# Two matrix products in seven blocks, and triangular inverses that move between array halves, in a two-block f32 network

## The chip, the cores and the metric

The program runs on one core of one Trainium2 chip, all in f32. The metric is the device time of one execution in microseconds (us). The kernel before took 2334.2, 2336.51 and 2338.58 us in three runs, median 2336.51. Engines are named as in the profile: PE is TensorE (PEld its weight loads), DVE is VectorE, ACT is ScalarE, POOL is GpSimd, SP is the engine that issues most transfers.

## The reference, cut to what matters

The network has two blocks, each of two layers, on 256 tokens of width 1024. The first block's layer is a feed-forward, a hybrid mixer and another feed-forward; the change touches the mixer:

```python
def rg_lru(u, w_a, b_a, w_x, b_x, lam):       # u: 256 x 1280, ten heads of 128
    r = sigmoid(u @ w_a per head + b_a); i = sigmoid(u @ w_x per head + b_x)
    log_a = -8.0 * r * softplus(-lam)
    a = exp(log_a)
    mult = sqrt(-expm1(2.0 * log_a))
    # h_t = a_t h_{t-1} + mult_t * (i_t u_t)
    ...
def hybrid_mixer(h, ...):
    ...
    y_pool = pool_mixer(u_pool, ...) @ w_pool_up                       # 512 -> 1024
    y_lru = (rg_lru(v, ...) * gelu(u_gelu)) @ w_lru_up                 # 1280 -> 1024
    return (g_pool * y_pool + g_lru * y_lru) @ w_out                   # 1024 -> 1024
```

The second block's first layer is a delta-rule recurrence with 16 heads of 64, run forwards and backwards over 256 context and 256 latent tokens:

```python
    def step(S, inp):                         # S: 64 x 64 for each head
        r_t, w_t, k_t, v_t, kk_t, a_t = inp
        sa = einsum("bhvk,bhk->bhv", S, kk_t)
        S = S * w_t - outer(sa, kk_t * a_t) + outer(v_t, k_t)
        return S, einsum("bhvk,bhk->bhv", S, r_t)
```

Its second layer is differential attention, which the change doesn't touch.

## The kernel before, in words

**First block.** Weights lie in one tensor in the order of use and come as slots of 16 tiles of 128 x 128 (1 MB, issued by SP) into a ring of 5. TensorE goes through them in that order and writes to 8 PSUM banks, which a list (`Order`, here `FIRST`) deals out by the place in the program; each entry names the engine that empties it. Three kinds of product stand there: plain ones (`st.product`, L704: one weight tile against 256 tokens), and in the feed-forwards products of 2 x 2 blocks of weight tiles in seven multiplications instead of eight, each with 128 tokens (L1080 the first matrix, L1141 the second). For these VectorE adds up four sums of weight tiles per slot (`sum_slot`, S1 to S4, L2373 to L2376) and three combinations of the data; `add_down` (L2532 to L2542) puts the seven results together and adds them into x. In the mixer all is plain: the order is the w_in columns, the gates' products by head (`gate_a`, `gate_x`), then `pool_up` (8 outputs of 4 products), `lru_up` (8 of 10), `w_out` (8 of 8). VectorE runs the recurrence head by head (`recurrence(h)`, L2594 to L2605) with the decay worked out from a tanh of ScalarE by a reciprocal, then adds up y.

**The scan of the second block.** 32 turns (`TURNS`): 8 pairs of heads, 4 groups each (`GROUPS`). A turn q takes for both directions two chunks of 64 tokens: four units u of (chunk, direction), for two heads h. Head h = 0 lives on partitions 0 to 63, h = 1 on 64 to 127 (`halves`), and all its products of 64 x 64 run in the quadrant of the array with these rows and these columns. In each turn a unit needs the inverse of a triangular 64 x 64 matrix. It starts from the Gram products (`first_gram`), which VectorE copies under a mask over ones laid by ScalarE (`begin_inverse` after `lay_ones`), and doubles in levels 1 to 5: `lower_product` (L1343, 8 products), VectorE's mask (`mask_lower`, L2814), `next_inverse` (L1354 and L1356, 16 products, 8 in level 5), ScalarE's copy back (`take_inverse`, L1992). Levels 1 and 2 of turn q+1 are done within turn q, beside the levels 3 to 5 of turn q. The chain of the state goes between them: for each of the two chunks k of the turn before `state_product` (L1421, L1433), VectorE's `take_z`, `solve`, ScalarE's `take_u`, `out_and_state` (L1447 to L1456), `update_state` and `take_o`. Also `stacked_gram` (L1330, L1331), once a turn, and three side tiles for the pair ahead or behind ("middle": in q = 0 mod 4 the `spread` of kk_norm, L1364; "kv": L1391; "end": `low_rank` L1377 or `by_head` L1371).

The order on each engine is written out by hand in one loop over q per engine; a wait holds up all that stands behind it there. Once a pair VectorE makes the decay sums of the next pair (`sum_decays`, L2726, behind `mask_lower(q, 5)`), and each turn it transposes the v squares (`turn_squares`, L2800 and L2805), which SP then writes to memory and reads back turned for the `kv` products of the next turn (its wait is on `v_landed`, L1387).

## Time and profile before

| | |
|---|---|
| runs | 2334.2, 2336.51, 2338.58 us |
| profiled execution | 2333.88 us, span 2331.8 us |
| PE busy | 2298.4 us, 99% |
| DVE busy | 1541.3 us, 66% |
| ACT busy | 547.4 us, 23% |
| the chain that ended last | PE 92%, DVE 3%, ACT 3%, DMA 1% |
| of that, lines of PE | L704 28%, L1080 21%, L1141 12%, L1354 3%, L1343 2%, L1356 2% |

The span is the time between the first and the last recorded instruction; the execution's own time is 2.1 us longer. An f32 matmul leaves two records. Matmuls overlap in the pipeline, so the mean duration of one says little, and the pace is read from starts. In the view of time a row is a run of like instructions: start, the time that they took together, their line and shape (rows*columns of the array, then the written tile), and in brackets the idle time before with what ended it.

### The profile page before, as it was taken

To read this page: it belongs to the slowest core of one execution; us is meant where nothing else is said; L and a number is where in the kernel's file an instruction comes from. 1 tells how busy PE (TensorE), PEld (TensorE's weight loads), DVE (VectorE), ACT (ScalarE), POOL (GpSimd) and SP (SyncE) were. 2 spreads that over 40 slices of the span, in tenths; PEclk is the share of its full clock that TensorE was granted. 3 is DMA by queue.
4 is the path that set the end of the run, shared out by engine and by line. 5 is a ranking of instruction groups with operands and counts; after the bars stand their busy time and mean duration, and the time that the engine had idled before them with its cause. 6 is when DMAs were issued, how large, how long until landed. Compare 5 with 4: busy or idle time off the path is not lost.

```text
span 2331.8 us, 55763 instructions
## 1 busy us (share of the span) xinstructions
PE 2298.4 (99%) x24340; PEld 2011.3 (86%) x24340; DVE 1541.3 (66%) x3133; ACT 547.4 (23%) x1280; POOL 413.9 (18%) x483
## 2 busy tenths in 40 slices
PE   8999999999999999999999999999999999999999
PEld 8999888899999998888999988668888889456558
DVE  7886775388768866671897887446666666147552
ACT  2101030111011000301110201225555554032341
POOL 1111000011111200000123440025445451100000
PEclk9999999999999999999999999999999999999999
DMA  7555454445545554544555421113333334212212
GB/s 284 195 181 192 171 197 145 163 166 195 200 170 192 182 199 145 217 151 158 184 194 181 145 91 73 37 27 62 61 59 59 60 61 100 98 56 89 73 37 73
DMA packets 169458, 310.29 MB, mean 133 GB/s; under 512 B 108992, under 2 KB 134768, under 8 KB 135296
## 3 DMA queue, kind: packets, MB, share of 16 engines
q1 hardware_dynamic: 165024, 278.02, 36.4%
q0 software_dynamic: 4192, 28.72, 3.4%
q8 instruction: 192, 3.15, 0.6%
q14 instruction: 50, 0.41, 0.1%
HBM read 293.06 MB, written 13.63 MB: 132 GB/s over the span
## 4 chain that ended last, share of the span: by engine, by line
PE 92%; DVE 3%; ACT 3%; DMA 1%; issue 1%; SPq 1%; POOL 0%; DVEq 0%; ACTq 0%; POOLq 0%
PE psum L704 28%; PE psum L1080 21%; PE psum L1141 12%; PE psum L1249 6%; PE psum L722 6%; PE psum L1354 3%; PE psum L1343 2%; PE psum L1356 2%; PE psum L1451 1%; PE psum L1051 1%; PE psum L1447 1%; PE psum L1377 1%; DVE arena L2814 1%; PE psum L1612 1%; PE psum L1654 1%
## 5 line engine op out<-in xcount | busy, mean ns | idle before, releaser
L704 PE MATMUL psum<-arena,ring 128*128 128x256 f32 (+1 forms) x2864 | 674.7, 395 | 8.3 <-ACT arena L1758 8.0
L704 PEld LDWEIGHTS psum<-arena,ring 128*128 128x128 f32 x2864 | 541.4, 190 | 129.5 <-issue 56.4
L1080 PE MATMUL psum<-arena 128*128 128x128 f32 x2560 | 325.0, 275 | 0.0
L1080 PEld LDWEIGHTS psum<-arena 128*128 128x128 f32 x2560 | 305.1, 192 | 0.0
L1080 PE MATMUL psum<-arena,ring 128*128 128x128 f32 x1920 | 253.6, 275 | 0.0
L1080 PEld LDWEIGHTS psum<-arena,ring 128*128 128x128 f32 x1920 | 233.9, 192 | 0.2
L2373 DVE TENSOR_TENSOR arena<-ring 128x1024 f32<-128x1024 f32 x136 | 171.0, 1258 | 38.7 <-PE psum L1141 34.8
L1141 PE MATMUL psum<-arena 128*128 128x128 f32 x1408 | 184.6, 275 | 0.0
L1141 PEld LDWEIGHTS psum<-arena 128*128 128x128 f32 x1408 | 170.7, 192 | 0.0
L1354 PE MATMUL psum<-arena 64*64 64x64 f32 x2560 | 162.1, 222 | 7.2 <-DVE arena L2814 5.3
L2395 DVE SCALAR_TENSOR_TENSOR arena<-arena 128x256 f32<-128x256 f32 x336 | 164.0, 529 | 5.1
L1354 PEld LDWEIGHTS psum<-arena 64*64 64x64 f32 x2560 | 142.7, 133 | 27.8 <-DVE arena L2814 17.9
L1141 PE MATMUL psum<-arena,ring 128*128 128x128 f32 x1056 | 146.0, 275 | 0.0
L722 PE MATMUL psum<-arena,ring 128*128 128x512 f32 (+1 forms) x336 | 137.9, 555 | 0.0
L1356 PE MATMUL psum<-arena 64*64 64x64 f32 x2048 | 134.8, 218 | 0.0
L1141 PEld LDWEIGHTS psum<-arena,ring 128*128 128x128 f32 x1056 | 131.4, 192 | 0.1
L2814 DVE TENSOR_TENSOR arena<-psum,arena 128x256 f32<-128x256 f32 x160 | 67.8, 424 | 88.4 <-PE psum L1343 83.9
L1783 ACT ACTIVATE arena<-arena 128x256 f32<-128x256 f32 x88 | 36.7, 417 | 370.3 <-DVE arena L2511 343.6
L1356 PEld LDWEIGHTS psum<-arena 64*64 64x64 f32 x2048 | 122.1, 135 | 0.0
L1992 ACT ACTIVATE arena<-psum 128x512 f32<-128x512 f32 x128 | 76.3, 597 | 150.6 <-PE psum L1356 149.9
L722 PEld LDWEIGHTS psum<-arena,ring 128*128 128x128 f32 x336 | 61.3, 189 | 53.6 <-issue 50.1
L1343 PE MATMUL psum<-arena 64*64 64x64 f32 x2560 | 104.8, 220 | 1.0 <-ACT arena L1992 0.9
(338 smaller groups left out, 3372.7 us busy)
## 6 DMA issues: line engine op xcount, KB each, us to landing
ring<-in_weights SPq DMA_DIRECT2D x238, 1024.0 KB, 4.8
arena<-in_ada POOLq DMA_DIRECT2D x24, 1024.0 KB, 5.2
squares<-arena SPq DMA_DIRECT2D x128, 96.0 KB, 2.1
arena<-squares SPq DMA_DIRECT2D x128, 64.0 KB, 2.8
arena<-squares SPq DMA_DIRECT2D x128, 32.0 KB, 2.3
arena<-in_const POOLq DMA_DIRECT2D x1, 1312.0 KB, 6.7
arena<-in_x SPq DMA_DIRECT2D x1, 1024.0 KB, 4.8
ring<-in_weights SPq DMA_DIRECT2D x2, 512.0 KB, 6.6
```

The source lines that it names most:

```text
L704: mm = self.nc.tensor.matmul(out, self.ring[:, slot % RING, i * P:(i + 1) * P], rhs, start=(kc == 0), stop=(kc == len(moving) - 1))
L722: mm = self.nc.tensor.matmul(out, self.ring[:, slot % RING, i * P:(i + 1) * P], rhs, start=start, stop=stop)
L1080: mm = nc.tensor.matmul(bank[:, n * P:(n + 1) * P], left[:, kind, pair, :], right[:, pair, :], start=(n == 0 and pair == 0), stop=(n == la ...
L1141: mm = nc.tensor.matmul(out_[name][:, n * P:(n + 1) * P], left[:, kind, place, :], right[:, pair, :], start=(n == 0 and pair == 0), stop=( ...
L1249: mm = nc.tensor.matmul(out_[:, n * T:(n + 1) * T], left[:, kind, pair, :], right[:, pair, :], start=(n == 0 and pair == 0), stop=(closes ...
L1343: mm = mm_(ps_t[b][halves[h], u, :], lt_all[halves[h], b, u, :], xy[halves[h], b, 0, u, :], start=True, stop=True)
L1354: mm = mm_(ps_xy[b][halves[h], 1, u, :], t_, y_, start=True, stop=True)
L1356: mm = mm_(ps_xy[b][halves[h], 0, u, :], y_, t_, start=True, stop=True)
L1992: ins = nc.scalar.activation(xy[:, b, :, :, :], ps_xy[b], ACT.Copy)
L2373: link(tt(sum_[:, S1:S3 + 1, :], w[:, W22:W11 + 1, :], w[:, W21:W21 + 1, :].to_broadcast([P, 2, QUADS * P]), ALU.add))
L2395: ins = stt(sum_, ada_[:, b, kc, :], weight, sum_, ALU.mult, ALU.add)
L2814: tt(t_low[:, b, :, :], ps_t[b], mask(f"below{level}"), ALU.mult).then_inc(s.t_masked[b], 1)
```

## The change

**The mixer's `lru_up` and `w_out`** are computed in seven multiplications for eight, as the feed-forwards' second matrices: 20 quadruples of weight tiles (2 x 2 tiles) for `lru_up`, 16 for `w_out`, four quadruples to a slot. VectorE makes nine more slot sums per layer (`sum_mixer_weights`), three combinations of hs, and per unit of two outputs those of y; the seven results of a unit of `lru_up` are put together in a new function `lru_up(unit)`, one of them copied by ScalarE first, those of `w_out` by `add_down`. The padding tiles of the mixer's weights stand ahead of `lru_up` and no longer behind `w_out`. ScalarE computes the decay a itself (an Exp for each head, ahead of the tanh), and `recurrence` is without its reciprocal and two TENSOR_SCALARs.

**The scan.** For odd q the inverses move: the result of a level is written to the other half's partitions (`half_of`), so its products have rows of one half and columns of the other, where those of even turns stay in their own. `first_gram` writes level 1 so; `begin_inverse` of an odd turn therefore copies the lower matrix twice, once to each half (two more copies of 64 x 256), and ScalarE's second laying of ones is twice as wide for it. A new `next_inverses` issues level 4 of turn q and level 1 of q+1 in alternation, and so level 5 and level 2. The order of the turn is new on TensorE, VectorE and ScalarE.

```diff
+    def half_of(q, level, h):
+        return h if q % 2 == 0 else (h + level) % 2
...
                 for u in range(4):
                     for h in range(2):
-                        mm = mm_(ps_t[b][halves[h], u, :], lt_all[halves[h], b, u, :], xy[halves[h], b, 0, u, :],
-                                 start=True, stop=True)
+                        at = halves[half_of(q, level, h)]
+                        mm = mm_(ps_t[b][at, u, :], lt_held[held][at, u, :], xy[at, b, 0, u, :], start=True, stop=True)
...
+            def inverse_product(q, level, i, u, h):
+                b, at, to = q % 2, halves[half_of(q, level, h)], halves[half_of(q, level + 1, h)]
+                y_, t_ = xy[at, b, 1, u, :], t_low[at, b, u, :]
+                left, right = (t_, y_) if i else (y_, t_)
+                return mm_(ps_xy[b][to, i, u, :], left, right, start=True, stop=True)
...
+            def next_inverses(q, level, level_ahead):
+                pe.wait_ge(s.t_masked[q % 2], level_count(q, level))
+                pe.wait_ge(s.t_masked[(q + 1) % 2], level_count(q + 1, level_ahead))
                 for u in range(4):
...
+                    for i in (1, 0):
+                        for h in range(2):
+                            if i or level < LEVELS - 1:
+                                mm = inverse_product(q, level, i, u, h)
+                        for h in range(2):
+                            mm_ahead = inverse_product(q + 1, level_ahead, i, u, h)
...
                     first_gram(q + 1)
+                lower_product(q, 3)
                 if k >= 0:
                     state_product(k)
-                lower_product(q, 3)
                 stacked_gram(q)
+                next_inverse(q, 3, range(0, 2))
                 if k >= 0:
                     solve(k)
-                next_inverse(q, 3)
+                next_inverse(q, 3, range(2, 4))
+                if ahead:
+                    lower_product(q + 1, 1)
                 if k >= 0:
                     out_and_state(k)
+                lower_product(q, 4)
                 side(q, "middle")
-                lower_product(q, 4)
                 if ahead:
-                    lower_product(q + 1, 1)
-                next_inverse(q, 4)
+                    next_inverses(q, 4, 1)
...
                 if k >= 0:
                     state_product(k + 1)
+                side(q, "kv")
+                lower_product(q, 5)
                 if ahead:
-                    next_inverse(q + 1, 1)
-                lower_product(q, 5)
+                    lower_product(q + 1, 2)
                 if k >= 0:
                     solve(k + 1)
-                side(q, "kv")
+                side(q, "end")
                 if ahead:
-                    lower_product(q + 1, 2)
-                next_inverse(q, 5)
+                    next_inverses(q, 5, 2)
...
                 if k >= 0:
                     out_and_state(k + 1)
-                side(q, "end")
-                if ahead:
-                    next_inverse(q + 1, 2)
...
+                if b:
+                    for h in range(2):
+                        nc.vector.copy_predicated(lt_held[2][halves[h], :, :], mask_bits("earlier")[halves[h], :, :],
+                                                  ps_first[b][halves[1 - h], 1, :, :])
...
-                    link(ts(scr[:, 0, :], t, 1.0, None, ALU.add))
-                    link(nc.vector.reciprocal(scr[:, 1, :], scr[:, 0, :]))
-                    ts(scr[:, 2, :], scr[:, 1, :], 2.0, -1.0, ALU.mult, ALU.add)
...
+                for i, units in enumerate(LRU_PLAN + OUT_PLAN):
+                    if i + SUM_BUFFERS - 1 < MIXER_SUMS:
+                        sum_mixer_weights(i + SUM_BUFFERS - 1)
+                    for unit, pairs in units:
+                        if i < len(LRU_PLAN):
+                            if pairs[-1][1] == LRU_PAIRS - 1:
+                                lru_up(unit)
+                        elif pairs[-1][1] == OUT_PAIRS - 1:
+                            add_down(unit, s.x_mixed, "w_out")
```

TensorE in a turn with q = 0 mod 4, from the last products of level 3 on. Before, L1354 and L1356 are the two products of `next_inverse`, L1447, L1451 and L1456 `out_and_state`, L1364 the side tile in the middle, L1343 `lower_product`:

```order
L1356 MATMUL psum<-arena 64x64
L1447 MATMUL psum<-ring,arena 64x64 x4
L1451 MATMUL psum<-arena 64x64 x4
L1456 MATMUL psum<-arena 64x64 x4
L1364 MATMUL psum<-arena 64x128 x8
L1343 MATMUL psum<-arena 64x64 x16
L1354 MATMUL psum<-arena 64x64
L1356 MATMUL psum<-arena 64x64
```

In the new kernel L1420 is `inverse_product`, L1412 `lower_product`, L1523 `solve`, L1537, L1541 and L1546 `out_and_state`, L1454 the side tile, L1511 `state_product`, L1481 the `kv` tile:

```order
L1420 MATMUL psum<-arena 64x64 x8
L1412 MATMUL psum<-arena 64x64 x8
L1537 MATMUL psum<-ring,arena 64x64 x4
L1541 MATMUL psum<-arena 64x64 x4
L1546 MATMUL psum<-arena 64x64 x4
L1412 MATMUL psum<-arena 64x64 x8
L1454 MATMUL psum<-arena 64x128 x8
L1420 MATMUL psum<-arena 64x64 x32
L1511 MATMUL psum<-arena,ring 64x64 x4
L1481 MATMUL psum<-arena 64x64 x8
L1412 MATMUL psum<-arena 64x64 x16
```

`lower_product(q+1, 1)` now stands ahead of `out_and_state`, and where two groups of 16 inverse products stood apart there is one of 32.

VectorE at the beginning of an odd turn's inverse, before: L2832 is `take_z`, L2814 the mask of level 3, L2786 and L2787 the copies under a mask of `begin_inverse`, L2822 the masks of the stacked Gram products, L2847 and L2860 `update_state`:

```order
L2832 TENSOR_TENSOR arena<-psum,arena 128x128
L2814 TENSOR_TENSOR arena<-psum,arena 128x256
L2786 COPY_PREDICATED arena<-arena,psum 128x512
L2787 COPY_PREDICATED arena<-arena,psum 128x256
L2822 TENSOR_TENSOR arena<-psum,arena 128x4x128 x2
L2814 TENSOR_TENSOR arena<-psum,arena 128x256
L2847 SCALAR_TENSOR_TENSOR arena<-psum,arena 128x64 x2
L2860 TENSOR_SCALAR arena<-arena 128x64 x2
```

And in the new kernel, where L2995 is `take_z`, L2977 the mask, L2944, L2948 and L2950 `begin_inverse`, L2985 the stacked masks:

```order
L2977 TENSOR_TENSOR arena<-psum,arena 128x256
L2995 TENSOR_TENSOR arena<-psum,arena 128x128
L2944 COPY_PREDICATED arena<-arena,psum 128x512
L2948 COPY_PREDICATED arena<-arena,psum 64x256 x2
L2950 COPY_PREDICATED arena<-arena,psum 128x256
L2977 TENSOR_TENSOR arena<-psum,arena 128x256
L2985 TENSOR_TENSOR arena<-psum,arena 128x4x128 x2
L2977 TENSOR_TENSOR arena<-psum,arena 128x256
L3010 SCALAR_TENSOR_TENSOR arena<-psum,arena 128x64 x2
L3023 TENSOR_SCALAR arena<-arena 128x64 x2
```

The two half copies are new (L2948), `take_z` comes behind the mask of level 3, and the mask of level 1 for the turn ahead comes right behind `begin_inverse`, ahead of the stacked masks.

## Rows read from the trace of the kernel before

**Rows 1.** The page: busy time by engine, and the granted clock in 40 slices.

```profile
PE 2298.4 (99%) x24340; PEld 2011.3 (86%) x24340; DVE 1541.3 (66%) x3133; ACT 547.4 (23%) x1280; POOL 413.9 (18%) x483
PEclk9999999999999999999999999999999999999999
```

**Rows 2.** The chain of waits in order of time: start, length, what ran.

```profile
318.33 138.75 PE psum L704 x640
...
466.18 125.06 PE psum L1080 x1120
```

**Rows 3.** View of time, PE, the scan: stacked Gram products that open a turn.

```profile
1661.37 0.32 PE L1331 MATMUL psum<-ring 64*64 64x128 f32 x1
...
1664.47 0.45 PE L1447 MATMUL psum<-ring,arena 64*64 64x64 f32 x8 [0.96 <-ACT arena L2005]
...
1676.17 0.32 PE L1331 MATMUL psum<-ring 64*64 64x128 f32 x1
...
1689.70 0.32 PE L1331 MATMUL psum<-ring 64*64 64x128 f32 x1
...
1717.47 0.32 PE L1331 MATMUL psum<-ring 64*64 64x128 f32 x1
```

**Rows 4.** View of time, DVE, feed-forward: a slot sum, and the end of `add_down`.

```profile
469.73 1.22 DVE L2373 TENSOR_TENSOR arena<-ring 128x1024 f32<-128x1024 f32 x1
470.98 0.69 DVE L2375 TENSOR_TENSOR arena<-arena,ring 128x512 f32<-128x512 f32 x1
...
663.71 0.42 DVE L2540 TENSOR_TENSOR arena<-arena,psum 128x256 f32<-128x256 f32 x1 [1.78 <-PE psum L1141]
...
664.37 0.41 DVE L2542 TENSOR_TENSOR arena<-arena,psum 128x256 f32<-128x256 f32 x1
```

**Rows 5.** View of time, ACT and DVE, the recurrence.

```profile
317.76 4.22 ACT L1822 ACTIVATE arena<-arena 128x256 f32<-128x256 f32 x10
...
329.74 1.75 DVE L2597 RECIPROCAL arena<-arena 128x256 f32<-128x256 f32 x1
```

**Rows 6.** View of time, PE: the tile kk_norm, and one level of an inverse.

```profile
1665.36 1.05 PE L1364 MATMUL psum<-arena 128*64 128x128 f32 x16
...
1682.44 0.34 PE L1354 MATMUL psum<-arena 64*64 64x64 f32 x4
...
1683.42 0.57 PE L1343 MATMUL psum<-arena 64*64 64x64 f32 x13
```

**Rows 7.** View of time, PE: stacked Gram products on all four quadrants.

```profile
1676.34 0.28 PE L1330 MATMUL psum<-ring 64*64 64x64 f32 x4
...
1676.55 0.27 PE L1331 MATMUL psum<-ring 64*64 64x128 f32 x1
```

**Rows 8.** View of time, ACT: what stands around the laying of ones.

```profile
1660.71 1.28 ACT L1934 ACT_TABLE_LOAD   x1
...
1663.17 0.63 ACT L1949 ACTIVATE arena<-arena 128x512 f32<-128x512 f32 x1
1663.68 0.41 ACT L1951 ACTIVATE arena<-arena 128x256 f32<-128x256 f32 x1
```

**Rows 9.** View of time, DVE: decay sums, transposes, `begin_inverse`.

```profile
1670.82 2.33 DVE L2726 TENSOR_TENSOR_SCAN arena<-arena 128x512 f32<-128x512 f32 x2
...
1673.38 0.44 DVE L2800 STREAM_TRANSPOSE arena<-ring 128x256 f32<-128x256 f32 x1
...
1677.51 0.75 DVE L2786 COPY_PREDICATED arena<-arena,psum 128x512 f32<-128x512 int32 x1 [0.55 <-ACT arena L1951]
1678.14 0.44 DVE L2787 COPY_PREDICATED arena<-arena,psum 128x256 f32<-128x256 int32 x1
```

**Rows 10.** View of time, PE and DVE: `kv` products, and the last transpose before them.

```profile
1627.91 0.47 PE L1391 MATMUL psum<-arena 64*64 64x64 f32 x9 [0.57 <-DMA arena<-squares]
...
1674.26 0.27 DVE L2805 STREAM_TRANSPOSE arena<-arena 128x128 f32<-128x128 f32 x1
...
1683.95 0.27 PE L1391 MATMUL psum<-arena 64*64 64x64 f32 x1
```

More of the change, by code:

```diff
@@ L195, with quad_plan @@
 assert DOWN_UNITS * DOWN_PAIRS % QUADS == 0
-def down_plan():
+def quad_plan(slots, pairs_of_unit):
     plan = []
-    for i in range(DOWN_SLOTS):
+    for i in range(slots):
         units = {}
         for place in range(QUADS):
-            unit, pair = divmod(i * QUADS + place, DOWN_PAIRS)
+            unit, pair = divmod(i * QUADS + place, pairs_of_unit)
             units.setdefault(unit, []).append((place, pair))
@@ L352, in first_order @@
                 o.add((lay, "pool_mix", m), "dve")
-        for name in ("pool_up", "lru_up", "w_out"):
-            for m in range(DC):
-                o.add((lay, name, m), "dve")
+        for m in range(DC):
+            o.add((lay, "pool_up", m), "dve")
+        for name in ("lru_up", "w_out"):
+            for unit in range(MIXER_UNITS):
+                o.add((lay, name, unit, "first"), "dve")
+                o.add((lay, name, unit, "second"), "dve")
         feed_forward(lay, "ffn2", 2 * lay + 1)
@@ L770, in build @@
     half_b = keep.take(4 * DC)
+    log_a = keep.take(LAYERS * LH)
     s_state = keep.take(2, HEAD)
@@ L1829, in _ @@
                     nc.scalar.activation(gl[:, m, :], gl[:, m, :], ACT.Sigmoid).then_inc(s.g_done, 1)
+                for unit in range(MIXER_UNITS):
+                    name = lay, "lru_up", unit, "first"
+                    act.wait_ge(s.bank_full, FIRST.full(name))
+                    if unit >= 2:
+                        act.wait_ge(s.lru_p1_added, lay * MIXER_UNITS + unit - 1)
+                    nc.scalar.activation(u_pad[:, unit % 2, PAD:PAD + P], psum[:, FIRST.bank(name), 0:P],
+                                         ACT.Copy).then_inc(s.lru_p1_copied, 1)
                 feed_forward("ffn2", 2)
@@ L2236, in _ @@
                 if lay == last:
-                    pool.wait_ge(s.dve_taken, FIRST.taken((last, "w_out", DC - 1)))
+                    pool.wait_ge(s.dve_taken, FIRST.taken((last, "w_out", MIXER_UNITS - 1, "second")))
                     pool.dma_start(xx[:, :, 0:T], ctx_in).then_inc(s.context_loaded, 16)
@@ new lines, in _ @@
+                forms_of([[hs_of[:, :, k, half, :] for half in range(2)] for k in range(2)],
+                         [hs_forms[:, i] for i in range(3)]).then_inc(s.hs_forms_ready, 1)
+                sum_mixer_weights(0)
+                for m in range(DC):
+                    pool_up(m)
+                    if m == DC // 2 - 1:
+                        sum_mixer_weights(1)
+                for i, units in enumerate(LRU_PLAN + OUT_PLAN):
+                    if i + SUM_BUFFERS - 1 < MIXER_SUMS:
+                        sum_mixer_weights(i + SUM_BUFFERS - 1)
+                    for unit, pairs in units:
+                        if i < len(LRU_PLAN):
[3 more added lines that the diff above has]
+                            add_down(unit, s.x_mixed, "w_out")
@@ L3035 @@
         part.extend(tiles(a["w_pool_up"][l]))
-        part.extend(tiles(a["w_lru_up"][l]))
-        part.extend(tiles(a["w_out"][l]))
         part.append(np.zeros((MIXER_PAD, P, P), np.float32))
+        part.extend(quadruples(tiles(a["w_lru_up"][l])))
+        part.extend(quadruples(tiles(a["w_out"][l])))
         feed_forward("ffn2")
```

198 lines of the change are left out of this document (148 added, 50 removed).

## The prediction, made before the changed kernel ran

> **What bounds the kernel now.** I read the page first. TensorE is busy for 99% of the span at the full granted clock, VectorE for 66%, ScalarE for 23% [rows 1]. So an edit pays only if it shortens TensorE's stream or a wait of it. Next I read the chain of waits in order of time, which tells two kinds of place apart. In the first block (to about 1310 us) it is TensorE alone in long unbroken pieces: 640 records in 138.75 us, 1120 in 125.06 [rows 2]. There the length is a count times a pace. An f32 product leaves two records, so a product with 256 moving columns costs 2 x 138.75/640 = 0.434 us, one with 128 columns 2 x 125.06/1120 = 0.2233 us. In the scan over 32 turns (1554 to 1990 us) the view of time shows short pieces and many hand-overs. Four turns last 56.10 us there: stacked Gram products begin at 1661.37, 1676.17, 1689.70 and, two turns on, 1717.47 [rows 3], so the turns take 14.80, 13.53 and twice 13.9 us. Real waits of TensorE there are few (0.96 us at 1664.47 is among the longest), but each level of an inverse is product, mask on VectorE, product, copy on ScalarE, so the other engines' order decides as soon as TensorE gets shorter.
>
> **The mixers' last products.** Per layer 80 + 64 = 144 products of 256 columns go, 144 x 0.4336 = 62.4 us. In come 36 quadruples x 7 = 252 products of 128 columns, 252 x 0.2233 = 56.3 us. Two layers: -12.2 us, all of it on the chain.
>
> What has to hide beside it, per layer: VectorE gets nine slot sums (1.25 from the start of the first addition to that of the second, then 0.73 twice: 2.7 us each), four units of adding and forming at about 4.4 us (14 links of 0.2 to 0.46 us, from the same operations at 128 and 256 columns), and four additions into x at 3.0 us [rows 4]. A slot of 28 products lasts 28 x 0.2233 = 6.25 us, and a sum with four fifths of a unit is 6.2 us. That is full, but the first sums are made during pool_up, some 9 us ahead, and by my count the lead only falls to 6. The tightest place is the change from lru_up to w_out: unit 3's forms are ready about 4.0 us after the last lru_up product, and the 21 products put ahead of the ones that need them last 4.7 us. I take 0; at worst 1 us a layer. Into the next feed-forward the chain is that of ffn2 into the second layer's ffn1, where x is ready 1.1 us after the products [rows 4] and the row of the chain shows no wait of weight. Slots are used every 6.25 us where it was 16 x 0.4336 = 6.94, as in the feed-forwards, where the same ring keeps up.
>
> The recurrence loses a reciprocal of 1.75 us [rows 5] and two short operations per head. ScalarE gets ten exponentials ahead of the tanh (4.2 us, like its ten Tanh [rows 5]), so the first root is 4.2 us later, 6.8 with two more table loads of 1.28 [rows 8]. TensorE runs eight banks ahead there, about 18 us, so both cost 0.
>
> **The scan: what leaves TensorE.** A turn has 16 products in each of the inverses' levels 1 to 4, 8 in level 5. On two quadrants 32 records take 0.98 us (1682.44 to 1683.42), 29 to 30 ns each [rows 6], so 58 ns per quadrant. Now level 4 of turn q runs with level 1 of q+1, and level 5 with level 2, on four quadrants. If the quadrants don't hinder each other, two of 0.93 us become one, and 0.47 + 0.93 becomes 0.93: -1.40 us a turn. No row shows four equal streams. The nearest is the stacked Gram: 11 records begin between 1676.33 and 1676.55 on all four quadrants, 20 ns each [rows 7]. At 20 ns the 64 records take 1.28 us. Bounds for the first merged group: 0.93 (free) and 1.87 us (no concurrency). I take 1.05, between free and the Gram's pace.
>
> **The scan: what comes late in its place.** I laid one turn out, with T the last record of the merged products that end the turn before. Hand-overs, as I read them off the starts of such pairs: 0.26 us from a last start to VectorE or ScalarE, 0.05 back. I go through a turn with q = 0 mod 4, like the one at 1661. ScalarE copies both inverses and the output and is free at T+1.4. Then come the gates of the pair ahead (table load and two, 2.45 us up to 1663.17) and the ones (0.52 + 0.41) [rows 8]; for an odd turn ahead the second lay is twice as wide, so it ends at T+5.0. VectorE then begins the odd inverse: 0.64 + 0.43 as before [rows 9], and two half-array copies, not shown before, between 0.1 and 0.44 each; I take 0.33, by the 128x256 one. That is done at T+6.8. The product that waits for it, lower_product(q+1, 1), stands now ahead of out_and_state(k), where TensorE arrives at T+4.7; before it stood one group (1.0 us) and a tile later. So here 2.1 us are waited, and behind it queue out_and_state (0.89 from 1664.47 to 1665.36 [rows 3, 6], and 0.15 for the switch of tile shape), lower_product(q, 4) 0.48, the tile kk_norm 1.1 [rows 6], and the merged products end at T+10.9. From there: state 0.24, kv, ScalarE's copy 0.26 + 0.60 + 0.05, two lower products 0.97, solve 0.24, the end tile 1.2, merged 0.95: 4.3 us. Total 15.2 against 14.80. The same count gives 13.5 against 13.9 for q = 2 mod 4 (exponentials of 1.3 us before the ones, no middle tile; wait for the stacked masks and the level-4 mask) and 13.5 against 13.9 for q = 3 (square root with its load ahead of the begin).
>
> For q = 1 mod 4 the inverses alone would allow 12.6. But in the turn before, the two decay scans (2.33 us) now stand behind the mask of level 2, and the transposes (1.15 us) behind them [rows 9]: squares_turned comes at T+1.7, where it now comes 0.1 us before the turn's start. The v squares go out to memory and back. In one turn TensorE waited 0.57 us for them (1627.91); in another they were there at most 9.4 us after the last transpose (1674.53 to 1683.95, no wait) [rows 10]. I take 8.7, a little under that, so T+10.4; TensorE would be at kv at T+8.8. It waits 1.6 us, of which 0.3 was stall anyway: 13.9 against 13.53.
>
> Four turns: 15.2 + 13.9 + 13.5 + 13.5 + 4 x 0.12 for the merged pace = 56.6 against 56.1; seven such groups +3.5, and the last pair, whose side tiles are missing, -2. The scan stays where it is, +1.5 us. Bounds: if v lands in time and the quadrants are free, 7 x -2.2 and -2, about -17; if neither, see the rivals.
>
> **Sum.** The profiled execution took 2333.88 us, its span 2331.8 and 2.1 around it. 2333.9 - 12.2 + 1.5 = 2323.2. It lay 2.6 us under the median of the three runs (2336.51, from 2334.2 to 2338.58), so the median should come to about 2325.
>
> A rule of the Trainium skill speaks against the merging. The page TensorE: Matmul & The Clock Gate, section "Wait — 56ns, not 53.3ns?", says "Start-to-start never drops below ≈25 ns however small N is". By it 64 merged records take 1.6 us and 48 take 1.2, so the scan would end 25 us later than in my sum and the kernel near 2350. The trace doesn't bear it out for f32 on quadrants (20 ns each over 11 records), but it has no such stretch longer than a microsecond.
>
> **Rivals.**
> - The scan gains too (0.20): v lands before kv, and the masks' chain is shorter than I count. For it: several of my waits overlap. Against: VectorE and ScalarE must do more in odd turns. 12 to 17 us less: 2308 to 2315.
> - Four quadrants don't run together (0.13), so that the change doesn't do what it says: TensorE issues at its present 29 ns. Then the pairs cost 1.87 and 1.40 us again, 1.3 us a turn more than in my sum, 31 turns: +40; part of it hides the waits I count, so 2345 to 2362, slower than before. It decides from about 23 ns per record: +0.42 + 0.17 us a turn is 18 us, which eats the mixers' gain. For it: no row shows the pace; against: the Gram rows.
> - The odd turn's begin costs more (0.13): ScalarE's queue ahead of the ones or the half copies are longer, by 0.3 to 0.6 us a turn: +9 to +19, so 2334 to 2344, about no change.
> - The mixers' gain is eaten by VectorE (0.06), which falls behind by 1 us a slot: 9 sums x 2 layers, 2330 to 2341.
>
> **Chances.** My forecast has 0.48, from 2318 to 2331. 0.2% is 4.7 us, about what a measurement can tell from no change. Faster by more (under 2331.8): the forecast, the first rival and a little of the last, 0.70. Within: most of the last two, 0.15. Slower: 0.15. The range is 2308 to 2340.
>
> **What would show it.** Right: pieces of 224 ns products, 56 us, where 62 us stood in both mixers, VectorE's sums well ahead; merged groups of 64 records in 1.0 to 1.1 us; a wait before lower_product(q+1, 1) in even turns of 0.4 to 2 us; kv waiting for a DMA in turns 1 mod 4; four turns in 56 to 57 us. Wrong: merged groups of 1.3 us or more, kv never waiting, four turns under 54 or over 58, or a wait between lru_up and w_out.

## The result: slower by 0.3%, and the profile after

The changed kernel takes 2343.0 us in the median (20 runs, 2336.57 to 2348.87), the kernel before 2334.19 (20 runs, 2331.39 to 2338.58): 1.0034 of the time before, 95% interval 1.0025 to 1.0042. Forecast were 2325 us and a range of 2308 to 2340. Its runs also lie farther apart, 12 us from the lowest to the highest for 7.

The first block gained what was forecast, all but half a microsecond. In the chain of waits of the changed kernel `quad_products` (L1214) stands in one piece in each layer, as long as worked out (56.3):

```profile
390.18 56.28 PE psum L1214 x504
...
1037.44 56.28 PE psum L1214 x504
```

The scan's first stacked Gram products begin at 1542.24 us for 1553.96 before, 11.7 us earlier. The scan lost it, and more: its 31 turns from there to the last stacked Gram take 445.6 us for 426.0. The page's busy row shows it from TensorE's side, with 97% of the span for 99% [rows 1]:

```profile
PE 2267.8 (97%) x24772; PEld 1989.1 (85%) x24772; DVE 1594.7 (68%) x3288; ACT 557.1 (24%) x1310; POOL 416.5 (18%) x483
```

The same four turns as in [rows 3], by the view of time of TensorE (L1398 is now `stacked_gram`): 57.45 us for 56.10.

```profile
1654.41 0.32 PE L1398 MATMUL psum<-ring 64*64 64x128 f32 x1
...
1669.93 0.32 PE L1398 MATMUL psum<-ring 64*64 64x128 f32 x1
...
1684.95 0.32 PE L1398 MATMUL psum<-ring 64*64 64x128 f32 x1
...
1711.86 0.32 PE L1398 MATMUL psum<-ring 64*64 64x128 f32 x1
```

What ends TensorE's waits, from the view of waits for TensorE alone over the scan (total, times, longest). Before:

```profile
PE psum L1447 <- ACT arena L2005: 6.0, 11, 1.0
PE psum L1354 <- DVE arena L2814: 4.7, 8, 1.3
PE psum L1391 <- DMA arena<-squares: 1.2, 2, 0.6
PE psum L1343 <- ACT arena L1992: 0.5, 1, 0.5
```

And after:

```profile
PE psum L1412 <- DVE arena L2950: 23.2, 18, 2.6
PE psum L1481 <- DMA arena<-squares: 17.8, 9, 3.1
PE psum L1420 <- DVE arena L2977: 8.4, 15, 1.0
PE psum L1397 <- issue: 2.5, 1, 2.5
```

12.4 us of waits have become 53 (with three small rows not shown). Two make it up: `lower_product(q+1, 1)` (L1412) waits for the last copy of `begin_inverse` (L2950), and the `kv` products (L1481) for the v squares. Turn 8 and turn 9 show both, and the merged group between them, in TensorE's view of time:

```profile
1659.15 0.68 PE L1412 MATMUL psum<-arena 64*64 64x64 f32 x16 [2.60 <-DVE arena L2950]
...
1662.25 1.16 PE L1420 MATMUL psum<-arena 64*64 64x64 f32 x64
1663.23 0.22 PE L1511 MATMUL psum<-arena,ring 64*64 64x64 f32 x2
...
1675.78 0.45 PE L1511 MATMUL psum<-arena,ring 64*64 64x64 f32 x8
1679.15 0.62 PE L1481 MATMUL psum<-arena 64*64 64x64 f32 x14 [2.92 <-DMA arena<-squares]
```

The merged group works: 64 records begin from 1662.25 on and the next product at 1663.23, 15 ns a record for the 29 of [rows 6]. The median over the scan is 0.94 us from first to last start. How the two waits arise stands on VectorE, whose rows answer to [rows 9] and [rows 10]:

```profile
1657.01 0.72 DVE L2944 COPY_PREDICATED arena<-arena,psum 128x512 f32<-128x512 int32 x1 [1.82 <-ACT arena L2055]
1657.75 0.89 DVE L2948 COPY_PREDICATED arena<-arena,psum 64x256 f32<-64x256 int32 x2
1658.65 0.44 DVE L2950 COPY_PREDICATED arena<-arena,psum 128x256 f32<-128x256 int32 x1
...
1665.65 2.33 DVE L2882 TENSOR_TENSOR_SCAN arena<-arena 128x512 f32<-128x512 f32 x2
...
1668.76 0.27 DVE L2968 STREAM_TRANSPOSE arena<-arena 128x128 f32<-128x128 f32 x1
```

VectorE stands idle for 1.82 us until ScalarE has laid the ones (L2055), and only then makes four copies; a half copy takes as long as one over all partitions (0.45 us). The transposes stand behind the decay sums and end at 1669.03. Then SP's queue sends the squares out and, 4.7 us later, fetches them:

```profile
1669.12 1.79 SPq L1052 DMA_DIRECT2D squares<-arena  x4
1673.79 6.36 SPq L1062 DMA_DIRECT2D arena<-squares  x8
```

The `kv` products wait for the first four of the eight fetches. These are back 10.0 us after the transposes, at 1679.0.

A third loss I had not thought of: the granted clock. The kernel before has it at 1.00 all through the scan. In the changed kernel it is at half in 8 of 31 turns (the profile's clock times the length of each turn gives 34.5 us at 1.2 GHz), each time behind one of these waits or the stall of L1397. Turn 20, one with a wait of 2.4 us that begins at 1830, by windows (PEclk is the third column from the end):

```profile
1831.00:1834.50 3.50, 2.11 (x36) 1.99 (x38) 2.25 (x6) 0.01 (x1) 0.00 (x0) 0.61 0.23 34
1834.50:1836.00 1.50, 1.50 (x28) 1.26 (x24) 0.68 (x2) 0.97 (x2) 0.00 (x0) 0.50 0.53 83
1836.00:1838.00 2.00, 2.00 (x22) 1.67 (x24) 0.81 (x3) 0.35 (x1) 0.00 (x0) 0.50 0.39 61
```

This turn takes 18.1 us, where turns 12 and 24 with much the same wait (2.6 us) and a full clock take 15.4. The Trainium skill (TensorE: Matmul & The Clock Gate, section "HAM oscillation — how this bites in real kernels") tells of a clock that falls to half when TensorE runs idle for want of data and costs time beyond the wait; this trace agrees, with idle pieces of 1.8 to 3.1 us ahead of such stretches, though not behind every one: of the scan's 12 idle pieces of 1.8 us or more, 8 are followed by half clock and 4 are not (turns 8, 9, 12 and 24).

The single runs point the same way. Of the changed kernel's 20 runs the five with a mean granted clock of 0.993 or more took 2336.6 to 2340.2 us, the ten with 0.991 or less 2341.1 to 2348.9. That alone doesn't show which is the cause, since a longer wait lengthens a run and lowers its clock.

### The profile page after: what moved, and what is told of

It is laid out like the page before. It is cut to its first block, busy times and chain, and to the rows that moved or that the text cites. A ratio compares the mean times of both kernels' runs of the same rounds, so it can differ in the third digit from the quotient of the medians.

```text
span 2340.9 us, 56946 instructions
## 1 busy us (share of the span) xinstructions
PE 2267.8 (97%) x24772; PEld 1989.1 (85%) x24772; DVE 1594.7 (68%) x3288; ACT 557.1 (24%) x1310; POOL 416.5 (18%) x483
## 4 chain that ended last, share of the span: by engine, by line
PE 87%; DVE 6%; DMA 3%; ACT 2%; SPq 2%; issue 1%; POOL 0%; DVEq 0%; POOLq 0%
PE psum L718 22%; PE psum L1115 21%; PE psum L1176 12%; PE psum L1315 6%; PE psum L736 6%; PE psum L1214 5%; PE psum L1412 3%; PE psum L1420 2%; DMA squares<-arena 1%; DMA arena<-squares 1%; SPq L1062 1%; PE psum L1086 1%; PE psum L1481 1%; DVE arena L2500 1%; PE psum L1705 1%
## 5 line engine op out<-in xcount | busy, mean ns | idle before, releaser
L718 PE MATMUL psum<-arena,ring 128*128 128x256 f32 (+1 forms) x2288 | 550.0, 399 | 9.2 <-DMA ring<-in_weights 8.9
L718 PEld LDWEIGHTS psum<-arena,ring 128*128 128x128 f32 x2288 | 432.0, 190 | 114.5 <-issue 57.4
L1115 PEld LDWEIGHTS psum<-arena,ring 128*128 128x128 f32 x1920 | 233.9, 192 | 0.2
L2478 DVE TENSOR_TENSOR arena<-ring 128x1024 f32<-128x1024 f32 x154 | 192.8, 1252 | 47.0 <-PE psum L1176 34.5
L1420 PEld LDWEIGHTS psum<-arena 64*64 64x64 f32 x4608 | 113.5, 137 | 35.8 <-issue 19.4
L2977 DVE TENSOR_TENSOR arena<-psum,arena 128x256 f32<-128x256 f32 x160 | 67.8, 424 | 106.5 <-PE psum L1412 104.9
L1420 PE MATMUL psum<-arena 64*64 64x64 f32 x4608 | 128.0, 225 | 9.4 <-DVE arena L2977 8.8
L1412 PE MATMUL psum<-arena 64*64 64x64 f32 x2560 | 109.0, 229 | 23.8 <-DVE arena L2950 23.2
L1176 PEld LDWEIGHTS psum<-arena,ring 128*128 128x128 f32 x1056 | 131.4, 192 | 0.1
L1412 PEld LDWEIGHTS psum<-arena 64*64 64x64 f32 x2560 | 91.8, 140 | 34.1 <-DVE arena L2950 25.9
L2480 DVE TENSOR_TENSOR arena<-arena,ring 128x512 f32<-128x512 f32 x154 | 111.9, 727 | 5.3
L2481 DVE TENSOR_TENSOR arena<-arena,ring 128x512 f32<-128x512 f32 x154 | 110.0, 715 | 5.3
L736 PEld LDWEIGHTS psum<-arena,ring 128*128 128x128 f32 x336 | 61.3, 189 | 53.6 <-issue 49.8
```

The costliest lines, as they stand in the source:

```text
L718: mm = self.nc.tensor.matmul(out, self.ring[:, slot % RING, i * P:(i + 1) * P], rhs, start=(kc == 0), stop=(kc == len(moving) - 1))
L736: mm = self.nc.tensor.matmul(out, self.ring[:, slot % RING, i * P:(i + 1) * P], rhs, start=start, stop=stop)
L1115: mm = nc.tensor.matmul(bank[:, n * P:(n + 1) * P], left[:, kind, pair, :], right[:, pair, :], start=(n == 0 and pair == 0), stop=(n == la ...
L1176: mm = nc.tensor.matmul(out_[name][:, n * P:(n + 1) * P], left[:, kind, place, :], right[:, pair, :], start=(n == 0 and pair == 0), stop=( ...
L1412: mm = mm_(ps_t[b][at, u, :], lt_held[held][at, u, :], xy[at, b, 0, u, :], start=True, stop=True)
L1420: return mm_(ps_xy[b][to, i, u, :], left, right, start=True, stop=True)
```

## The experiments

Mean length in us of the turns 4 to 27 by q mod 4, from the starts of their first stacked Gram products, with the median of the runs, and the ratio to the kernel before, measured in the same job (with its 95% interval). The changed kernel ran in one job only, and the medians of the kernel before lay between 2334.2 and 2336.6 us in the five jobs, so a difference of two medians is good to 2 us at best:

```
kernel         0     1     2     3    sum    median    ratio to before
before       14.60 13.75 13.82 13.76  55.9
changed      15.89 15.32 13.87 13.13  58.2  2343.0   1.0034 (1.0025 to 1.0042)
mixers_only  14.60 13.66 13.80 13.76  55.8  2323.88  0.9960 (0.9945 to 0.9974)
scan_only    15.61 16.12 13.86 13.27  58.9  2361.03  1.0117 (1.0100 to 1.0134)
sq_first     15.61 12.59 13.83 13.27  55.3  2326.07  0.9962 (0.9948 to 0.9975)
ones_first   13.52 14.68 13.87 13.32  55.4  2325.84  0.9962 (0.9947 to 0.9977)
both_first   13.53 12.73 14.05 13.38  53.7  2309.87  0.9887 (0.9867 to 0.9907)
warm         15.46 14.56 14.16 13.35  57.5  2338.24  1.0008 (0.9997 to 1.0019)
apart        16.93 14.17 14.66 13.76  59.5  2347.20  1.0042 (1.0027 to 1.0057)
same_half    16.98 14.17 15.31 14.46  60.9  2362.54  1.0114 (1.0097 to 1.0131)
copies_sb    14.04 14.47 16.68 12.98  58.2  2337.19  1.0008 (0.9995 to 1.0022)
best         13.10 12.96 14.66 13.18  53.9  2313.51  0.9910 (0.9895 to 0.9924)
l1_late      16.94 15.53 16.39 15.75  64.6  2383.80  1.0201 (1.0181 to 1.0221)
before_ones  14.60 13.80 13.24 13.76  55.4  2332.57  0.9986 (0.9976 to 0.9996)
copies_act   13.94 15.10 12.98 13.21  55.2  2319.27  0.9933 (0.9909 to 0.9957)
both_apart   14.08 12.33 14.17 13.77  54.4  2317.88  0.9925 (0.9904 to 0.9947)
best_act     12.97 12.54 13.17 13.15  51.8  2303.31  0.9866 (0.9844 to 0.9888)
```

**The two parts alone.** `mixers_only` is the kernel before with the mixers' hunks of the change, `scan_only` with the others.

> The kernel before with the mixers' part of the change alone (lru_up, w_out in seven products, decay by Exp); the scan as before. Theory A (the whole gain of the change is here and the scan loses 20 us): 12 us less than before, about 2322; the scan's turns stay 14.8, 13.5, 13.8, 13.9 us. Rival B (the new layout of the mixers shifts what the scan starts from, so part of the scan's loss is theirs): less than 8 us faster.

> The kernel before with the scan's part of the change alone. Theory A: the scan's 32 turns take 446 us for 426, so about 20 us more than before, 2354. If the two parts are not additive (rival B), it lies more than 4 us off.

The mixers are worth 10.5 us between the medians (12.2 forecast), and their scan's turns are those of before: theory A. The scan alone costs 26.7 us, where 19.1 would make the sum of the parts: outside theory A, and rival B holds. Its trace has kv waits of up to 3.6 us in turns 1 mod 4, and 33.6 us at half clock, but its 31 turns take only 1.7 us longer than the changed kernel's (447.3 for 445.6). Of the rest, its scan begins 1.4 us later than in the kernel before, and behind its last turn it takes 2.7 us longer. Why it is worse alone than behind the new mixers no run settles.

**The v squares.**

```diff
-                if q % GROUPS == 0 and q // GROUPS + 1 < PAIRS:
-                    sum_decays(q // GROUPS + 1)
                 if ahead:
                     turn_squares(q + 1)
+                if q % GROUPS == 0 and q // GROUPS + 1 < PAIRS:
+                    sum_decays(q // GROUPS + 1)
```

> The changed kernel, with VectorE's transposes of the v squares ahead of the next pair's decay sums (turn_squares and sum_decays change places). Theory A: the round trip of the v squares is anchored to the transposes; they come 2.3 us earlier, so the wait ahead of the kv products in turns 1 mod 4 falls from 2 to 3.4 us to under 1, the granted clock there stays at 1.0, these turns take 12.7 to 13.2 us for 15.4, and the kernel is 15 to 18 us faster than the changed one: about 2326. Rival C (the round trip takes longer because of what else uses the queues there; or what needs the decay sums comes late in its place): less than 8 us. Rival D (the clock falls for other reasons than the waits): waits gone but clock still 0.9 in these turns, 8 to 11 us.

16.9 us faster than the changed kernel, turns 1 mod 4 at 12.6. TensorE's waits show that one alone fell, and the half clock there is gone (three stretches are left, two behind the other wait and one in turn 30 behind a stall that the profile puts down to nothing, "issue"):

```profile
PE psum L1412 <- DVE arena L2950: 21.5, 17, 2.6
PE psum L1420 <- DVE arena L2977: 9.0, 17, 1.0
PE psum L1481 <- DMA arena<-squares: 5.3, 8, 1.5
```

**The ones.** `lay_ones(q + 2)` goes from the head of turn q+1 to the end of turn q, ahead of `side_tail`:

```diff
-                if 2 <= q + 1 < TURNS:
-                    lay_ones(q + 1)
...
+                if q + 2 < TURNS:
+                    lay_ones(q + 2)
                 side_tail(q)
```

> The changed kernel, with ScalarE's laying of ones for turn q+2 put at the end of turn q ahead of the gates and exponentials, where it now stands at the head of turn q+1 behind them. Theory A: in turns 0 mod 4 the ones are ready 2.5 us earlier, the odd begin_inverse is done at about 4.9 us after the last merged product, and the wait ahead of lower_product(q+1, 1) falls from 2.6 us to 0.3 to 0.6; in turns 2 mod 4 from 1.2 to about 0.2. Per four turns 3 us less, and no drop of the clock behind that wait (turns 16, 20): 20 to 27 us faster than the changed kernel, 2316 to 2323. Rival E (VectorE's own queue or the Gram products set the beginning, not the ones): the wait falls by under 1 us and the kernel gains under 8 us.

17.2 us faster. The turns 0 mod 4 are 13.52 us, all but to the hundredth, and the wait there is 0.72 us:

```profile
1763.31 0.51 PE L1412 MATMUL psum<-arena 64*64 64x64 f32 x10 [0.72 <-DVE arena L2950]
```

Less than the 20 to 27 us forecast: the turns 2 mod 4 did not gain at all (13.87 for 13.87; `copies_act` below shows that VectorE's half copies hold them up), and half clock behind waits for the squares is left in four turns. The same move in the kernel before:

> The kernel before the change with the same move of the ones ahead of the gates. Theory A (there the ones are not what TensorE waits for: lower_product(q+1, 1) stands a group and a tile later): within 3 us of the kernel before. Rival N (the ones' place costs the kernel before as much): 10 us or more faster.

2.3 us between the medians (interval of the ratio 0.9976 to 0.9996): theory A. In the kernel before no product waits for `begin_inverse` in the view of waits, and its turns 0 mod 4 stay at 14.60, so there the late ones are a wait that the change made. They were not free before, though: its turns 2 mod 4 fall from 13.82 to 13.24 us, and the wait of 0.4 to 0.5 us for a mask (L1354 <- L2814) in them is gone.

**Both.**

> The changed kernel with both orders: v squares transposed ahead of the decay sums, and ones laid ahead of the gates. Theory A (two separate waits, each with its share of the half clock): the gains add, 17 + 17 us, so 2307 to 2312; four turns take 13.5 + 12.8 + 13.8 + 13.2 = 53.3 us, no stretch at half clock. Rival G (with the shorter turn 0 mod 4 the squares are late again, as both waits hid in one another): 2315 to 2322, with kv waits of 1 to 2 us in turns 1 mod 4.

2309.87, 33.1 us below the changed kernel, for 16.9 and 17.2 apart: the gains add, theory A. Half clock is left in two turns (1 and 30), where none was expected.

**The clock by itself.** Repeated products fill the waits; they write again the values that are there.

```diff
+                if ahead and k >= 0 and q % GROUPS == 0:
+                    for _ in range(5):
+                        for u in range(2, 4):
+                            for i in (1, 0):
+                                for h in range(2):
+                                    inverse_product(q, 3, i, u, h)
                 next_inverse(q, 3, range(2, 4))
...
-                for d in range(2):
+                for d in list(range(2)) * (10 if k % 2 == 1 and (k // 2 + 1) % GROUPS == 1 else 1):
```

> The changed kernel, with TensorE given repeated products while it would wait: in turns 0 mod 4 the second half of next_inverse(q, 3) is issued five more times (about 2.3 us), in turns 1 mod 4 state_product(k+1) ten times for once (2.2 us more); same values written again, so the waits' ends stay where they are. Theory A (the half clock follows on the idle time and costs extra): no stretch at half clock in the turns 0 and 1 mod 4 from turn 5 on, turns 0 mod 4 all at 15.4, turns 1 mod 4 at 14.5 to 15.3, so 5 to 10 us faster than the changed kernel, 2333 to 2338. Rival H (the half clock costs nothing, since other engines set the pace there): within 2 us of the changed kernel or slower. Rival I (the clock doesn't follow the idle time): the stretches at half clock stay.

The time at half clock fell from 34.5 to 6.8 us (turns 1 and 29), and the kernel is faster with more work: 4.8 us between the medians, 6 by the ratios (1.0034 and 1.0008, whose intervals leave 3 to 9). So theory A, against H and I, though not to the letter: turn 29 is a turn 1 mod 4 and went to half clock behind a stall that the profile puts down to "issue". Turn 20 of this kernel over two of the windows shown above:

```profile
1831.00:1834.50 3.50, 3.29 (x104) 3.09 (x102) 2.53 (x6) 1.03 (x4) 0.00 (x0) 1.00 0.32 51
1834.50:1836.00 1.50, 1.50 (x40) 1.36 (x38) 1.50 (x4) 1.11 (x2) 0.00 (x0) 1.00 0.45 65
```

This is less than what the clock costs, since in turns with early squares the repeated products delay `kv`: turn 13 takes 15.02 us here for 12.68 in the changed kernel, at full clock in both.

**What the merging is worth.** `apart` issues the two halves of a merged group one after the other; `same_half` leaves the alternation and keeps every inverse in its quadrants (and reads the lower matrix from there):

```diff
-                    next_inverses(q, 4, 1)
+                    next_inverse(q, 4)
+                    next_inverse(q + 1, 1)
```

```diff
-                return h if q % 2 == 0 else (h + level) % 2
+                return h
```

> The changed kernel with its halves and order, but the merged groups issued one after the other (level 4 of q, then level 1 of q+1; level 5, then 2). Theory A (four quadrants run together only when products alternate between them): two groups of 32 records at 29 ns are 1.87 us for 1.0, and 1.4 for 0.95: 1.3 us more in each of 31 turns, a part of it behind waits: 25 to 42 us slower than the changed kernel, 2368 to 2385. Rival J (the merging doesn't save what is counted, something else gives the pace): less than 10 us.

> The changed kernel with its order and its alternating issue, but every inverse stays in its own quadrants (half_of gives h; the two half copies are still made and not used). Theory A (it is the four quadrants that let records begin every 15 ns): 64 records on two quadrants take 1.87 us again, 25 to 42 us slower than the changed kernel. Rival K (alternation alone does it, by independent products): the groups keep 1.0 us and the time stays at 2343.

From first to last start, a group of 64 records takes 0.94 us in the changed kernel, 1.69 in `apart`, 1.86 in `same_half`; one of 48 takes 0.94, 1.22 and 1.40 (medians). So both are needed, four quadrants and alternation, and together they bring all that could be had: two streams that don't hinder each other. The same group in `same_half`, and the next in `apart` (58 of 64 records in its row):

```profile
1711.01 2.08 PE L1420 MATMUL psum<-arena 64*64 64x64 f32 x64
```

```profile
1721.47 1.73 PE L1420 MATMUL psum<-arena 64*64 64x64 f32 x58
```

But in the kernel's time `apart` costs 4.2 us between the medians, 2 by the ratios (hardly clear of nothing), and not 25 or more: theory A's pace was right, its path wrong, and rival J holds. `same_half` costs 19.5 us, also under its 25; why so much more than `apart`, whose groups are only 0.2 us shorter, no run settles. Do the waits swallow the gain?

> The kernel with both orders (squares first, ones first), its merged groups issued one after the other. In the changed kernel that cost only 4 us, though the groups took 1.69 and 1.22 us for 0.94 and 0.94. Theory A (there the 1.0 us a turn that the merging saves was spent in waits that end by themselves, at the v squares above all): with these waits gone the same edit costs 0.8 to 1.1 us in each of 31 turns, 24 to 34 us more than 2310. Rival P (the merged groups were never on the path for more than a few us): again under 10 us.

With both waits mended the same edit costs 8.0 us between the medians, 9 by the ratios (whose intervals leave 2 to 15, so 24 is out): rival P. By kind of turn it is 0.55, -0.40, 0.12 and 0.39 us, so the waits for the squares in turns 1 mod 4 still swallow a part, and only a part. ScalarE's rows show the rest. When the groups are apart, it copies level 4 while TensorE is at the second group, and stands ready for the second copy 0.16 us early:

```profile
1764.32 0.60 ACT L2096 ACTIVATE arena<-psum 128x512 f32<-128x512 f32 x1 [1.40 <-PE psum L1420]
1765.08 0.60 ACT L2096 ACTIVATE arena<-psum 128x512 f32<-128x512 f32 x1 [0.16 <-PE psum L1420]
```

When they are merged (`both_first`, the same turn), both copies begin after the end:

```profile
1760.37 1.08 ACT L2094 ACTIVATE arena<-psum 128x512 f32<-128x512 f32 x2 [1.40 <-PE psum L1420]
```

From the group's first product to the next `lower_product` it is 2.05 us apart (1763.12 to 1765.17) and 1.84 merged (1759.17 to 1761.01): of 0.75 us saved, 0.21 arrives. It is 0.2 in nearly all the turns 0 and 2 mod 4, and 0.5 in nearly all with 3 mod 4 (2.34 and 1.85 us).

**The place of lower_product(q+1, 1)**, put back right ahead of the merged group:

> The changed kernel with lower_product(q+1, 1) moved behind out_and_state(k), lower_product(q, 4) and the side tile, right ahead of the merged products. Theory A (its place costs 2.8 us in turns 0 mod 4, but its mask has to be done before the merged products): wait of 2.8 us gone in turns 0 mod 4, they take 0.5 to 1 us less; in the other turns the mask stands directly ahead of the merged group and costs 0.5 to 1.5 us: on the whole 5 to 25 us slower. Rival M (the place alone is the fault): 15 us faster, like with the ones laid first.

41 us slower, the sign right and the size far under-counted: in every turn the merged group now waits 2.1 us for a mask, and the clock is at half for 79 us in 17 turns. The early place was needed for the merging.

**The half copies**, behind the signal that the inverse has begun and in SBUF, first by VectorE (`copies_sb`, and `best` with both orders), then by ScalarE behind `take_o(k)` (`copies_act`, and `best_act`, the same lines with `nc.scalar.activation`). In all four ScalarE also lays only as many ones as before the change:

```diff
-                        nc.vector.copy_predicated(lt_held[2][halves[h], :, :], mask_bits("earlier")[halves[h], :, :],
-                                                  ps_first[b][halves[1 - h], 1, :, :])
...
+                        nc.vector.tensor_copy(lt_held[2][halves[h], :, :], lt_held[1][halves[1 - h], :, :])
```

> The changed kernel, with the odd turns' second lower matrix made behind the signal that the inverse has begun: two copies of 64x256 in SBUF from half to half (the first matrix is ready then), for two masked ones of 64x256 from PSUM ahead of it; ScalarE lays only as many ones as before the change. Theory A (the half copies stand on the path in every even turn, at 0.45 us each and not 0.33): begin_inverse is done 0.9 us earlier where the ones are not what it waits for, a little more in turns 0 mod 4 (0.2 us shorter laying): 0.9 to 1.1 us in each of 15 turns, 12 to 17 us faster than the changed kernel, 2326 to 2331. Rival L (something else of VectorE or the squares' round trip ends the wait): under 6 us.

> The changed kernel with all three: squares transposed before the decay sums, ones before the gates, half copies behind the signal. Theory A: the waits are separate, so 12 to 15 us less than with both orders (2310): 2295 to 2299, four turns in 51.5 us. Rival G (the squares' round trip takes over as turns get shorter): kv waits above 1 us in two of four turns, 2303 to 2308.

`copies_sb` gains 5.8 us where 12 to 17 were expected, and `best` is 3.6 us slower than `both_first` where it was to be 12 to 15 faster. The turns 0 mod 4 did gain (14.04 for 15.89), those with 2 mod 4 lost 2.8 us. VectorE's rows say why, in a turn 0 and in a turn 2 mod 4 of `copies_sb`:

```profile
1654.63 0.59 DVE L2949 COPY arena<-arena 64x256 f32<-64x256 f32 x2
...
1798.83 2.52 DVE L2949 COPY arena<-arena 64x256 f32<-64x256 f32 x2
```

Two copies take 0.59 us in the one, where GpSimd is idle, and 2.52 in the other, where it is busy all through. It is so all over this scan: 0.29 us for each of the 18 copies with GpSimd idle, 0.5 to 1.3 for the 14 with GpSimd busy. With ScalarE as the one that copies:

> The changed kernel, with the odd turns' second lower matrix copied from half to half by ScalarE behind its copies of the turn's first outputs (two Copy of 64x256), no longer by VectorE. In the run with VectorE's copies in SBUF these took 0.29 us each in turns 0 mod 4 and 1.2 us each in turns 2 mod 4, where GpSimd works for 12.7 of 13.7 us; there turns 0 mod 4 were 1.3 us shorter and turns 2 mod 4 2.5 us longer. Theory A (VectorE's copy is slowed by GpSimd's work, and the half copies stood on the path): turns 0 mod 4 at 14.1 to 14.3, turns 2 mod 4 at 12.9 to 13.2, no wait above 0.5 us ahead of the merged group of 64: 12 to 18 us faster than the changed kernel, 2325 to 2331. Rival O (turns 2 mod 4 are bound by the stacked masks and the mask of level 4, whoever copies): 2 mod 4 at 13.7, under 9 us.

> The changed kernel with squares before decay sums, ones before gates, and the half copies on ScalarE. Theory A: 2296 to 2302; four turns in 12.9 + 12.7 + 13.1 + 13.2 = 51.9 us. Rival G (the squares' round trip takes over): 2303 to 2308, with kv waits above 1 us in more than a third of the turns.

`copies_act` is 23.7 us faster than the changed kernel, turns 0 mod 4 at 13.9 and 2 mod 4 at 13.0: theory A, and more than its 12 to 18 us. The rest I put to fewer stretches at half clock (17.0 us for 34.5 in the profiled executions), which is argued from one trace each. `best_act` is the fastest, 0.9866 of the kernel before (0.9844 to 0.9888), 31 us less; its turns take 51.8 us for four, as expected, its time is 1 us over, and kv waits above 1 us stand in 2 of the 24 turns, so the round trip has not taken over (rival G), though it is now what TensorE waits for most (11.4 us over the scan, a good part of it in the turns 1 to 3 and 29).

## Why the prediction was wrong

**Mixers: right.** 56.3 us a piece worked out, 56.28 measured; the sum -12.2 against -11.7 in the trace and -10.5 between medians. TensorE has no wait within the `quad_products`, and what VectorE's sums and ScalarE's exponentials cost is at most the half microsecond that is missing. The rival in which VectorE falls behind is out.

**The quadrants: right, and better.** 1.05 us taken for the first merged group, 0.94 measured. The rival of no concurrency is out, and so is the rule of the Trainium skill weighed there (TensorE: Matmul & The Clock Gate, section "Wait — 56ns, not 53.3ns?"): 15 ns from record to record over 64 of them, for its ≈25 ns. It is not borne out for products on different quadrants.

**The size of the scan: wrong, +1.5 forecast, +19.6 measured in the trace.** By kind of turn, forecast with 0.12 added for the merged pace and then measured (with before's mean): 15.3, 15.89 (14.60); 14.0, 15.32 (13.75); 13.6, 13.87 (13.82); 13.6, 13.13 (13.76). The mechanisms named were the ones that came: a wait ahead of `lower_product(q+1, 1)` in even turns, `kv` waiting for a DMA in turns 1 mod 4. Three terms failed:

- *The half clock was no term of the sum.* The step that failed is "So here 2.1 us are waited": a wait was priced at its own length. In the trace waits grew by 40.6 us (12.4 to 53.0), and the merging took the 1.4 us a turn that the prediction counts off TensorE's stream, 31 x 1.4 = 43 (32 records take 0.98 us before, the merged groups 0.94). The scan still lost 19.6, so 22 us are left: 15 of them in the 8 turns with half clock, 7 in the other 23. Six of the 8 can be held against a turn of their kind at full clock (16 and 20 against 12; 5, 17, 21 and 25 against 9, less the difference of their waits). They are 9.8 us longer for 24 us at half clock, so my estimate for all 34.5 us is 14, most of the 18 by which the scan's sum was off. At full clock the count nearly holds: turns 8, 12 and 24 take 15.4 to 15.5 us for 15.3. By experiment the clock is shown to be worth 5 to 6 us or more (`warm`); the 14 rest on the trace alone. The 7 us beside it show in no wait; the hand-overs behind a merged group, which took most of its gain in `both_first`, are the likely place, not a shown one.
- *"I take 8.7" for the round trip of the squares.* In the turns 1 mod 4 from 5 to 25 it took 9.45, 9.98, 7.52, 9.34, 9.92 and 8.58 us (mean 9.1, in the whole scan 7.5 to 12.0), and from the start of TensorE's last product to that of `kv` it was 2.89, 3.14, 0.97, 2.78, 3.36 and 2.02, so 2.5 on the mean for the 1.6 forecast. The squares' place was right (T+1.6 for T+1.7), TensorE was there at T+8.3 for T+8.8, and `kv` began at T+10.9 for T+10.4: 0.5 us a turn by this term, the rest of those turns' 1.3 us is the clock. Before the change the trip took much the same (7.6 to 10.2 us in these turns) and only two waits for it show, 1.2 us in all. That its scatter makes the kernel's runs lie farther apart is not shown: with the squares first, `both_first` still spreads over 10.6 us in four runs.
- *"I take 0.33, by the 128x256 one" for a half copy*: 0.45 each. In turn 8 `begin_inverse` is done at T+7.1 for T+6.8 and TensorE is there at T+4.3 for T+4.7, so the view has a wait of 2.6 us, which begins at the end of the record before, and not of 2.1. In turns 2 mod 4, where the forecast saw other things as the limit, the same copies cost 0.9 us (13.87 against 12.98 in `copies_act`, which also lays fewer ones).

Beyond the four-turn count, the first four turns lost 3.5 us and the last three 2.3, where 2 were to be gained; in turn 30 TensorE stands 2.53 us amid its stacked Gram for nothing that the profile names ("issue"), and the half clock follows. The traces of `sq_first`, `ones_first`, `both_first` and `copies_act` have the same stall, of 2.4 to 3.5 us. What makes it was not tried.

The range missed by 3 us. The chances erred more: "the scan gains too" had 0.20, "the odd turn's begin costs more" 0.13 with up to 2344. The latter's range holds the measured time, but by luck: what it names made turns 0 mod 4 longer by 0.1 us and turns 2 mod 4 by 0.3, some 3 us over the scan. The clock, on which no rival stood, brought the rest with the squares' scatter.

## What to carry to other kernels

A wait on TensorE costs more than its length where the clock follows (here behind 8 of 12 idle pieces of 1.8 to 3.1 us): price it with a stretch at half pace behind it, and mend waits before streams. Merged streams save only what their successors' hand-over doesn't take: two groups one after the other hide the copy of the first, so 0.75 us saved at the products became 0.2 to 0.5. And when operations move, look at what now stands ahead of the start of a long transfer: here one swap of two calls on VectorE was worth 17 us, one on ScalarE the same.

## What the runs showed of the hardware beyond that

- The records of 64x64 products in f32 (two a product) begin every 15 ns when the products alternate between two pairs of quadrants, every 29 ns on one pair.
- VectorE's copy of 64x256 in SBUF takes 0.29 us with GpSimd at rest and mostly 1.2 to 1.3 with GpSimd busy (`copies_sb`); ScalarE's takes 0.42 either way (`copies_act`). Masked copies from PSUM at that place of the changed kernel's turns take 0.44 to 0.46 with GpSimd busy or not.
- A masked copy over 64 partitions takes as long as over 128 (0.45 and 0.44 us for 256 elements).
